# The final RMSNorm of a two-layer encoder trunk, applied per token after the transposes instead of before them

## The reference, cut to what matters

```
def rms_norm(x, g):
    y = x * rsqrt(mean(x * x, axis=-1, keepdims=True) + EPS)
    return y * g
...
    # last lines of layer 1, then the end
    h = modulate(rms_norm(x, norm_ffn_g[l]), sh2, sc2)
    x = x + g2 * ((gelu(conv3(h @ w_gate)) * (h @ w_up)) @ w_down)   # w_down: 2816 x 1024
return rms_norm(x, final_g)                                          # (1, 512, 1024)
```

## Time and profile before

| | |
|---|---|
| median of 3 runs | 1386.04 us (1385.17 to 1388.10) |
| profiled execution | 1386.23 us |
| its span, from first to last instruction | 1384.4 us |
| TensorE busy | 1329.0 us (96%) |
| VectorE, ScalarE busy | 812.9 us (59%), 556.0 us (40%) |
| mean granted TensorE clock | 0.98 of full |
| data moved | 160.37 MB, of which 2.10 MB are written at the end |

### The profile page before, as it was taken

One profiled execution on the slowest core, in us unless ns is written; L12 is line 12 of the kernel. 1 busy time (PEld: TensorE's weight loads), 2 busy tenths in 40 slices (PEclk: granted clock), 3 DMA queues, 4 the chain that ended last, 5 costly groups with the idle time before them and its releaser, 6 DMA issues.

```text
span 1384.4 us, 17294 instructions
## 1 busy us (share of the span) xinstructions
PE 1329.0 (96%) x6220; PEld 1085.0 (78%) x6220; DVE 812.9 (59%) x1198; ACT 556.0 (40%) x837; POOL 47.3 (3%) x93
## 2 busy tenths in 40 slices
PE   4799997899999999999999999999999999999998
PEld 4677776686888888888878888887778888888785
DVE  6565356666666656545678777775775554552323
ACT  5455464424333333212255555553343333332213
POOL 1000000000000000000100000000000000000000
PEclk8899998999999999999989999999999999999999
DMA  9333432052554454464822222223523333332232
GB/s 360 117 110 89 122 111 73 1 158 86 151 148 141 149 153 136 138 194 147 266 78 68 70 76 76 62 62 102 173 76 106 91 94 103 91 99 99 80 102 76
DMA packets 189268, 160.37 MB, mean 116 GB/s; under 512 B 4960, under 2 KB 164921, under 8 KB 189219
## 3 DMA queue, kind: packets, MB, share of 16 engines
q1 hardware_dynamic: 177008, 116.41, 28.0%
q0 software_dynamic: 11936, 43.14, 10.0%
q10 hardware_dynamic: 274, 0.16, 0.0%
HBM read 157.59 MB, written 2.10 MB: 115 GB/s over the span
## 4 chain that ended last, share of the span: by engine, by line
PE 89%; DVE 5%; ACT 3%; DMA 2%; SPq 1%; issue 1%; DVEq 0%; ACTq 0%
PE proj L1451 61%; PE z L1451 22%; PE obank L1451 3%; PE misc L1451 2%; DMA w_raw<-ab_w_in 2%; SPq L450 1%; ACT w_hi L567 0%; DVE soft L1087 0%; DVE normed L957 0%; PE z L1888 0%; DVE hT_lo L963 0%; ACT q_sb L664 0%; DVE w_lo L924 0%; DVE hT_lo L1070 0%; PE z L1623 0%
## 5 line engine op out<-in xcount | busy, mean ns | idle before, releaser
L1451 PE MATMUL proj<-hT_hi,w_hi 128*128 128x512 f32 x1136 | 452.6, 398 | 10.9 <-DVE hT_lo L1070 4.7
L924 DVE TENSOR_TENSOR w_lo<-w_raw,w_hi 128x1024 fp32r<-128x1024 f32 x192 | 235.0, 1224 | 360.8 <-ACT w_hi L567 360.8
L1451 PE MATMUL proj<-hT_hi,w_lo 128*128 128x512 f32 x1136 | 444.8, 392 | 0.0
L1451 PE MATMUL proj<-hT_lo,w_hi 128*128 128x512 f32 x1136 | 444.5, 391 | 0.0
L567 ACT ACTIVATE w_hi<-w_raw 128x1024 fp32r<-128x1024 f32 x192 | 203.4, 1060 | 472.2 <-PE proj L1451 281.6
L1451 PEld LDWEIGHTS proj<-hT_hi,w_hi 128*128 128x128 f32 x1136 | 214.6, 189 | 65.1 <-issue 13.1
L1451 PEld LDWEIGHTS proj<-hT_hi,w_lo 128*128 128x128 f32 x1136 | 214.5, 189 | 45.7
L1451 PEld LDWEIGHTS proj<-hT_lo,w_hi 128*128 128x128 f32 x1136 | 214.8, 189 | 44.5 <-issue 1.7
L1451 PE MATMUL z<-gated_hi,w_hi 128*128 (+1 forms) x264 | 105.5, 400 | 0.1
L1451 PE MATMUL z<-gated_hi,w_lo 128*128 (+1 forms) x264 | 103.4, 392 | 0.0
L1451 PE MATMUL z<-gated_lo,w_hi 128*128 (+1 forms) x264 | 103.0, 390 | 0.0
(11 more groups left out here) (274 smaller groups left out, 1550.9 us busy)
## 6 DMA issues: line engine op xcount, KB each, us to landing
ada_raw<-ada_w POOLq DMA_DIRECT2D x80, 512.0 KB, 4.3
w_raw<-ffn_w_gate SPq DMA_DIRECT2D x44, 512.0 KB, 3.8
w_raw<-ffn_w_up SPq DMA_DIRECT2D x44, 512.0 KB, 4.0
w_raw<-ffn_w_down SPq DMA_DIRECT2D x44, 512.0 KB, 3.8
w_raw<-hg_w_in SPq DMA_DIRECT2D x32, 512.0 KB, 4.0
w_raw<-ab_w_in SPq DMA_DIRECT2D x18, 512.0 KB, 4.5
ada_first<-ada_w SPq DMA_DIRECT2D x7, 1024.0 KB, 17.2
w_raw<-ab_w_out SPq DMA_DIRECT2D x8, 512.0 KB, 4.7
```

Of the source, the lines that this page charges most:

```text
L924: nc.vector.tensor_tensor(w_lo[:, slot, :], w_raw[:, slot, :], w_hi[:, slot, :].bitcast(F32), ALU.subtract).then_inc(lo_done, 1)
L1451: return nc.tensor.matmul(dst, weights_ap, moving, start=start, stop=stop, skip_group_check=True)
```

## The change

The per-feature factor `final_g` and the per-token factor `rstd` are separated. VectorE multiplies each block by `final_g` alone (`final_scale`) as soon as the block is there, and TensorE transposes these unnormalised blocks (`final_transposes`). For blocks 0 to 3 that is done in the second half of the down projection: VectorE's four scales stand behind its split of unit `u0+HALF+2`, TensorE's 16 transposes (4 token blocks x 4 feature blocks, into `zb[2]`, `zb[3]`, `obank` and `misc`) behind unit `u0+HALF`, and ScalarE copies `misc` to `out_nat` behind its split of unit `u0+HALF+2`. Blocks 4 to 7 follow after the last unit, into `proj` and `zb[0]`, `zb[1]`.

The sums of squares are now taken with the squares as the stationary operand and one column of ones as the moving one (`final_sums`): 4 matmuls of one column for each of three tiles, which give a column of 128 tokens for each token block. The first four (from `sumsq`) stand ahead of the last group (3, 1) of `last_two`. Ln and Exp work on 128x4. At the end ScalarE evacuates features 0 to 511 and VectorE 512 to 1023 of each token block, multiplied by the token's `rstd`, and SyncE stores token block after token block (4 stores of 512 KB, rows of 4 KB). The output buffer is `ada_sum`, the scaled blocks lie in `ada_raw` and `h32`.

```diff
--- before.py
+++ after.py
@@ -109,7 +109,7 @@
     + ["mod3", "mod4", "norm1", "mod5", "mod6", "mod7", "mod8", "norm2"]
...
        for name in [f"key{p}", f"kv{p}", f"osq{p}"]]
-    + ["norm3", "norm4"]
+    + ["norm3", "fin"]
 )
@@ -240,6 +240,7 @@
             oT_lo = sb("oT_lo", [P, DC, SEQ], F32R, s1)
...
         starts = rstd
+        fin_rstd = rstd
...
         q_odd = [normed[:, 0, LINE:LINE + SEQ], normed[:, 1, LINE:LINE + SEQ], sumsq[:], rstd[:]]
@@ -252,8 +253,8 @@
             with ExitStack() as sf:
...
                 gated_lo.append(sb(f"gated_lo{layer}", [P, FB, SEQ], F32R, sf))
-        with ExitStack() as send:
-            out_nat = sb("out_nat", [P, TB, D], F32, send)
+        out_nat = ada_sum
+        fin_x = [ada_raw[:, dc // 2, 512 * (dc % 2):512 * (dc % 2) + 512] for dc in range(6)] + [h32[:, 0, :], h32[:, 1, :]]
...
         proj = [bank("proj0"), bank("proj1")]
@@ -266,6 +267,7 @@
...
         down_banks = [[zb[0], zb[1], zb[2], zb[3]], [proj[0], proj[1], zb[0], zb[1]]]
+        fin_banks = [[zb[2], zb[3], obank, misc], [proj[0], proj[1], zb[0], zb[1]]]
...
         p_bufs = [q_sb[:].rearrange("p a n -> p (a n)"), soft_a, weights]
@@ -377,7 +379,10 @@
         down_full = sem("down_full")
...
         fin_full = sem("fin_full")
-        fin_evac = sem("fin_evac")
+        fin_sum = sem("fin_sum")
+        fin_log = sem("fin_log")
+        fin_act = sem("fin_act")
+        fin_dve = sem("fin_dve")
...
         bias_col = small[:, 0, 0:96]
@@ -498,11 +503,10 @@
             ffn_units(1, U_FFN1)
...
-            out_view = out[0].rearrange("(t p) d -> p t d", p=P)
-            for k in range(4):
-                sp.wait_ge(fin_evac, 2 * k + 2)
-                sp.dma_start(out_view[:, :, 2 * k * P:(2 * k + 2) * P],
-                             out_nat[:, :, 2 * k * P:(2 * k + 2) * P]).then_inc(out_done, 16)
+            for i in range(TB):
+                sp.wait_ge(fin_act, i + 1)
+                sp.wait_ge(fin_dve, i + 1)
+                sp.dma_start(out[0, i * P:(i + 1) * P, :], out_nat[:, i, :]).then_inc(out_done, 16)
             sp.wait_ge(out_done, 64)
@@ -801,6 +805,9 @@
                     squares(n, q)
...
                 split(u0 + HALF + 2, 1)
+                if last:
+                    act.wait_ge(misc_full, MISC_AT["fin"] + 1)
+                    nc.scalar.activation(out_nat[:, TB - 1, 0:512], misc[:], ACT.Copy).then_inc(misc_free, 1)
                 with act.Fori(0, HALF // 2 - 1) as i:
...
                         split(u0 + HALF + 3 + 2 * i + s, s)
@@ -809,8 +816,7 @@
                 if not last:
...
                     split(u0 + FB + 1, 1)
-                root(n)
-                if not last:
+                    root(n)
                     modulated(n)
...
             out_units(U_OUT0, 1)
@@ -902,11 +908,17 @@
             down(U_DOWN1, 4, last=True)
...
-            for dc in range(DC):
-                act.wait_ge(fin_full, dc + 1)
-                nc.scalar.activation(out_nat[:, :, dc * P:(dc + 1) * P],
-                                     zb[dc % 4][:].rearrange("p (t n) -> p t n", t=TB), ACT.Copy
-                                     ).then_inc(fin_evac, 1)
+            act.wait_ge(fin_sum, 1)
+            nc.scalar.activation(fin_rstd[:, 0:TB], misc[:, 0:TB], ACT.Ln, bias=EPS, scale=1.0 / D).then_inc(fin_log, 1)
+            act.wait_ge(fin_log, 1)
+            nc.scalar.activation(fin_rstd[:, 0:TB], fin_rstd[:, 0:TB], ACT.Exp, scale=-0.5).then_inc(rstd_done, 1)
+            act.wait_ge(rstd_done, 4)
+            for i in range(TB):
+                src = fin_banks[0][i][:] if i < TB - 1 else out_nat[:, i, 0:512]
+                if i == 0:
+                    act.wait_ge(fin_full, 1)
+                nc.scalar.activation(out_nat[:, i, 0:512], src, ACT.Copy, scale=fin_rstd[:, i:i + 1]
+                                     ).then_inc(fin_act, 1)
...
         @block.vector
@@ -1256,6 +1268,12 @@
                 chain[0] += 2 * FB
...
             def down(u0, n, gate, last=False):
+                def final_scale(dc):
+                    dve.wait_ge(x_new, 8 * n + dc + 1)
+                    nc.vector.tensor_scalar(fin_x[dc], xT[:, dc, :], fin_g[:, dc:dc + 1], None, ALU.mult
+                                            ).then_inc(fin_y, 1)
                 def half_out(half, u):
...
                         dc = 4 * half + q
@@ -1267,9 +1285,17 @@
                                                        scalar=mod[:, gate, dc:dc + 1], in1=xT[:, dc, :],
...
-                        if q:
+                        if last and half:
+                            if q == 1:
+                                for d in range(dc - 1, dc + 1):
+                                    final_scale(d)
+                                    add_squares(n, d)
+                            elif q > 1:
+                                final_scale(dc)
+                        elif q:
                             add_squares(n, dc - 1)
-                    add_squares(n, dc)
+                    if not (last and half):
+                        add_squares(n, dc)
...
                     with dve.Fori(0, HALF // 2) as i:
@@ -1285,6 +1311,8 @@
                 split(u0 + HALF + 1, 0)
...
                 if last:
+                    for dc in range(4):
+                        final_scale(dc)
                     with dve.Fori(0, HALF // 2 - 1) as i:
...
                             split(u0 + HALF + 3 + 2 * i + s, s)
@@ -1435,13 +1463,10 @@
...
             dve.wait_ge(rstd_done, 4)
-            for dc in range(DC):
-                if dc >= 2:
-                    dve.wait_ge(fin_full, dc - 1)
-                nc.vector.scalar_tensor_tensor(out=h32[:, dc % 2, :], in0=xT[:, dc, :],
-                                               scalar=fin_g[:, dc:dc + 1], in1=rstd[:],
-                                               op0=ALU.mult, op1=ALU.mult).then_inc(fin_y, 1)
+            for i in range(TB):
+                dve.wait_ge(fin_full, 2 + i)
+                nc.vector.tensor_scalar(out_nat[:, i, 512:D], fin_banks[1][i][:], fin_rstd[:, i:i + 1], None,
+                                        ALU.mult).then_inc(fin_dve, 1)
...
         @block.tensor
@@ -1761,6 +1786,9 @@
...
                     for q, part in ((0, 0), (1, 0), (0, 1), (1, 1), (2, 0), (3, 0), (2, 1), (3, 1)):
+                        if layer and banks is down_banks[1] and (q, part) == (3, 1):
+                            pe.wait_ge(ss_done, 5 * n)
+                            final_sums(sumsq[:], True)
                         if q == 0:
...
                         sl = (slot + part) % 2
@@ -1776,6 +1804,22 @@
                         elif part == 1:
...
+                def final_sums(src, first=False):
+                    if first:
+                        misc_wait("fin")
+                        pe.wait_ge(misc_free, MISC_AT["fin"] + 1)
+                    for i in range(TB):
+                        last = mm(misc[:, i:i + 1], src[:, i * P:(i + 1) * P], ones[:, 0:1], start=first and i == 0)
+                    return last
+                def final_transposes(part, blocks, dcs):
+                    for i in blocks:
+                        for dc in dcs:
+                            at = (dc % 4) * P
+                            last = nc.tensor.transpose(fin_banks[part][i][:, at:at + P],
+                                                       fin_x[dc][:, i * P:(i + 1) * P], ident)
+                    return last
                 pe.wait_ge(gp_lo, FB * (layer + 1) - 1)
...
                 one(u0 + 1, 1, 2, mod_group=(6, None)[layer])
@@ -1786,11 +1830,30 @@
                 pe.wait_ge(gp_lo, FB * (layer + 1))
...
                 one(u0 + HALF, 1, 0, first=True, mod_group=(8, None)[layer], banks=down_banks[1])
+                if layer:
+                    pe.wait_ge(fin_y, 4)
+                    pe.wait_ge(gap_free, 2)
+                    misc_wait("fin")
+                    final_transposes(0, range(TB - 1), range(4)).then_inc(fin_full, 1)
+                    final_transposes(0, range(TB - 1, TB), range(4)).then_inc(misc_full, 1)
                 with pe.Fori(0, HALF // 2 - 1) as i:
...
                 last_two(u0 + FB - 2, 0, FB - 4, down_banks[1])
-                norm_sum(n)
+                if not layer:
+                    norm_sum(n)
+                    return
+                pe.wait_ge(sq_done, 8 * (n - 1) + 7)
+                final_sums(square[:, 0, :])
+                pe.wait_ge(fin_y, 6)
+                final_transposes(1, range(2), range(4, 6))
+                pe.wait_ge(sq_done, 8 * n)
+                final_sums(square[:, 1, :]).then_inc(fin_sum, 1)
+                pe.wait_ge(fin_y, DC)
+                for i in range(2):
+                    final_transposes(1, range(i, i + 1), range(6, DC)).then_inc(fin_full, 1)
+                for i in range(2, TB):
+                    final_transposes(1, range(i, i + 1), range(4, DC)).then_inc(fin_full, 1)
...
```

(8 more changed lines are left out.)

## The result

The changed kernel takes 1390.08 us (median of 10 runs, 1386.06 to 1391.30), the kernel before beside it 1386.26 us (10 runs). The ratio is 1.0025, with a 95% interval of 1.0016 to 1.0033: 3.5 us slower, between 2.2 and 4.6. The forecast was +3.35 us. The profiled execution took 1391.3 us with a span of 1389.5, so this one profile is about 1 us above its median; its sums are made within the span.

The account below looks back on a forecast made before the run. The prediction took TensorE, 89% of the chain of waits, to bound the kernel. It summed +7.2 mid-projection, +0.9 sums and -4.75 tail to +3.35 us: 1389.4 us against the 1386.04 median, range 1386.0 to 1391.9.

Parts of the forecast that it names:

- Step 1: Half boundary of the last down projection: TensorE waits for four final scales before the 16 transposes, losing 3.6 us.
- Step 2: Half boundary: the 16 transposes take 1.7 us plus 0.2 for starting up and going back, 1.9 us lost.
- Step 3: Half boundary, after the wait: TensorE's granted clock drops to half over the transposes, costing 1.7 us, bounds 0 to 3.3.
- The second stretch: Mid-projection: another half-clock stretch following the first, +1.7 us; part of a slower rival with chance 0.15.
- Step 4: Ahead of the last down group (3,1): four one-column fp32 sums delay TensorE by 0.9 us.
- Step 5: Tail from last down matmul to span end: 11.05 us instead of 15.8, with earlier, faster stores; -4.75 us.
- The held clock: Rival at the transposes: clock holds or drops in the idle at no cost; 1387.7 us, chance 0.22.
- The short stall: Rival at the half boundary: scales ready when TensorE arrives, mid-projection cost 1.9 us, no clock drop; 1384.1 us, chance 0.08.
- the delay that is made up elsewhere: Rival in the projection: weights set the pace, so the boundary delay never reaches the end; 1382.2 us, chance 0.05.
- the third rival: Two half-clock stretches at the transposes, or stores at 343 GB/s with scales at 692 ns; 1391.1 us, chance 0.15.

Follow-up runs that it names:

- E4: Changed kernel with VectorE's four final scales before its split of unit HALF+2 instead of behind it; ratio 1.0007 to the kernel before.
- E2: Changed kernel with the 16 transposes one down unit later on TensorE, behind unit HALF+1; ratio 0.9987 to the kernel before.
- E3: Changed kernel with 15 discarded 512-column matmuls on TensorE while it waits for the scales; ratio 1.0017 to the kernel before.
- E5: E4 plus 15 transposes of a constant in TensorE's wait, making its program 30 instructions longer; ratio 0.9986 to the kernel before.
- E7: Changed kernel without early transposes or misc copy, all 32 transposes behind the last down matmul; ratio 0.9967 to the kernel before.
- E9: E2 timed once more, same program, on another chip; ratio 0.9985 to the kernel before, median 1383.85 us.
- E10: E7 timed once more, on the same chip as E9; ratio 0.9978 to the kernel before, median 1382.40 us.
- E1: The changed kernel once more, unedited, with another profile; ratio 1.0027 to the kernel before.
- E8: Changed kernel with the third and fourth store issued by ScalarE's queue instead of SyncE's; ratio 1.0017 to the kernel before.
- E11: E10 with the first four one-column sums behind the last down matmul, all transposes after the sums; ratio 0.9971 to the kernel before.
- E6: E2 with the first four sums behind the last down matmul and transposes of blocks 4 to 7 after all sums; ratio 0.9969 to the kernel before.

## Why the prediction was right, and which term was mis-sized

*Step 1, the wait: right.* Predicted are 3.6 us from the old restart to the first transpose; in the profile 4.05 us of idle replace the 0.6 of before, 3.4 more. The scales took 1.67 us (1.8 predicted). E4 shows that the order on VectorE is the cause of half of it, the scales being most of the rest.

*Step 2: right.* 1.66 to 1.72 us for 16 transposes and the way back at full clock in E2, E3 and E4; 1.9 predicted.

*Step 3: right.* A half-clock stretch over just the transposes; 1.56 us by E3, 1.7 predicted. Whole projection: +6.7 us instead of +7.2. The second stretch did not come: after a stretch that held only transposes the clock was 1.00 from 1321.0, as after 1378.0 in the earlier trace rows. By the rule of the Trainium skill (TensorE: Matmul & The Clock Gate, Part 4: PE-mode transpose) it would have stayed low; the trace disagrees a second time. What decides whether an idle brings such a stretch, the prediction did not say; 4.05 us did, E4's 2.00 did not.

*Step 4: right,* 0.81 + 0.09 = 0.9 us.

*Step 5: the mis-sized term.* Predicted -4.75 us, profiled -3.1. Up to the first store it holds (X'+3.88, predicted 3.75), and without the load the whole does: the tails of E2, E3, E5, E7, E9 and E10 are 10.8 to 10.9 us, where 10.85 stood before I added 0.2 for the clock, which didn't fall there. What was missing is the load of TensorE's instructions on one of the DMA engines, +1.9 to +2.2 us; the prediction had no term for it. The stores' rate was right: 5.3 us for 2.10 MB predicted, 5.34 measured in E2 and E5, 393 GB/s. The figure of about 358 GB/s that the prediction took from the Trainium skill (HBM Reference, Specifications) is there the share of a core when both cores of an HBM domain stream; for a core that streams alone the same section gives about 425. The measured 393 lies between.

*Luck in the number.* The forecast of +3.35 us met the timed +3.5 almost exactly, and that is luck in part. By the rows the projection cost 0.5 us less than predicted and the tail gained 1.7 less, so they sum to +4.5; the timed runs lie 1.0 us below that, and this distance hides the missing term. *What stays open:* whether the load costs less in executions that aren't profiled. The three kernels that have it with the full wait are all timed below their sums, but E4, which has it too, is not, and moving the load away gained 2.9 us in the timed runs of E5, where the profiles say 2.2.

*The rivals.* The held clock was false for this kernel and became true in E3 and E4 by an edit. The short stall and the delay that is made up elsewhere are refuted by 4.05 us of idle and 53.3 us of full TensorE after it. Of the third rival neither half came true: there was one half-clock stretch, and the stores ran at over 343 GB/s.

## What to carry to other kernels

An operation that is moved "under" another stage lies in three programs at once: ask what stands before it on each engine, and place the consumer at least one unit behind the producer. Here one down unit decided the sign, from +0.25% to -0.14%: 5.2 us of that is the unit's own, and 1.9 us came because the longer program moved the instruction load away from the stores. Before work is moved early at all, look at what binds the end: the stores were bound by the rate of their data, so 16 transposes gained nothing by being early (E7). And when a tail is 2 us longer than its own rows explain, look at every DMA queue in that window, the instruction queue too.

## What the runs showed of the hardware

A 16 KB instruction load among the stores made one DMA engine late, and whoever waits for all 16 engines waits for that one. The load took 1.5 to 1.9 us on its engine in the four kernels that have it there (changed, E1, E4, E8), the last data came 1.4 to 2.0 us after the others at 18 to 39 GB/s, and the tail was 1.9 to 2.2 us longer. In none of the seven tails of 10.8 to 11.0 us is there a load among the stores. That load and late data lie on the same engine is inferred from this; the traces do not number the engines. Meanwhile a store's issue was held for 1.9 to 2.2 us, on either queue (changed kernel and E4, E8), in E1 two for 0.8 and 1.3 us. Where the load falls depends on the length of TensorE's program: 30 instructions more moved it from among the stores to some 2.5 us before the end of the last down matmul (E5), and in E3 the same 30 moved it as far. The Trainium skill (Runtime: NRT & Kernel Launch, Instruction fetch mechanics) says that the sequencer fetches blocks of 16 KiB over a DMA queue of its own and that the cost is mostly hidden; the size agrees with the rows, and in this tail the cost wasn't hidden.

Stores with rows of 4 KB ran at 393 GB/s over all their data where no load disturbed them (E2, E5), those with rows of 1 KB at 343 while they flowed. No run changed the row size alone.

An idle of 2.0 us brought no half clock (E4), one of 4.05 us did in all three profiles of it. Filling it with matmuls prevented it (E3). In E11 24 one-column instructions in a row, with TensorE busy all the time, were followed by half clock, as in the course of 32 at 699.42 in the earlier trace rows; in E6 the same 24 were not.
